# Three products of zeros ahead of each pass of the second expert layer, and the transposes of modulation sums half a piece later

## What is computed

```python
# first network, 256 tokens, four layers
for i in range(4):
    mod = cond @ ada_w[i] + ada_b[i]
    sh_a, sc_a, g_a, sh_f, sc_f, g_f = jnp.split(mod, 6, axis=-1)
    ...
    h = modulate(rms_norm(x, norm_g[i, 2]), sh_f, sc_f)
    y = jnp.square(jax.nn.relu(h @ ffn_w1[i])) @ ffn_w2[i]      # 1024 -> 4096 -> 1024
    x = x + g_f[:, None, :] * rms_norm(y, norm_g[i, 3])

# second network, expert layer (layer 0: 512 tokens, layer 1: 256 tokens)
def moe_ffn(h, w_router, e_bias, w_gate, w_up, w_down, s_gate, s_up, s_down):
    scores = jax.nn.sigmoid(h @ w_router)
    _, idx = lax.top_k(scores + e_bias, 8)
    ...
    def expert_block(args):
        tok, e = args
        xb = h_pad[tok]
        a = jax.nn.silu(xb @ w_gate[e]) * (xb @ w_up[e])        # 1024 -> 256
        return a @ w_down[e]                                    # 256 -> 1024
    ...
    return routed + shared
```

## Time and profile before

| | us |
|---|---|
| median of 3 runs | 3370.06 |
| the three runs | 3374.06, 3370.06, 3365.59 |
| the profiled execution's own time | 3373.5 |
| its span, first to last instruction | 3371.8 |
| PE busy | 3187.8 (95%) |
| DVE busy | 1277.8 (38%) |
| mean DMA rate | 255 GB/s |
| mean granted TensorE clock | 0.985 |

### The profile page before, as it was taken

One profiled execution on the slowest core, in us unless ns is written; L12 is line 12 of the kernel. 1 busy time (PEld: TensorE's weight loads), 2 busy tenths in 40 slices (PEclk: granted clock), 3 DMA queues, 4 the chain that ended last, 5 costly groups with the idle time before them and its releaser, 6 DMA issues.

```text
span 3371.8 us, 39704 instructions
## 1 busy us (share of the span) xinstructions
PE 3187.8 (95%) x14310; PEld 2152.6 (64%) x14310; DVE 1277.8 (38%) x3018; ACT 546.3 (16%) x1148; POOL 401.6 (12%) x462
## 2 busy tenths in 40 slices
PE   7999999999999999999999999998999998899897
PEld 5878878888888888888664434443445575333333
DVE  4766534565014565476442322222212033111112
ACT  3300122001021003200031211111112022111011
POOL 0000120001010000000220222221113001010000
PEclk9999999999999999999999999999999999999999
DMA  8687625774435773466300699999995216999996
GB/s 317 256 305 299 256 108 200 290 290 156 153 122 222 292 284 112 175 251 259 114 26 21 258 383 378 357 389 360 362 338 201 77 38 277 409 416 414 395 398 247
DMA packets 135329, 860.25 MB, mean 255 GB/s; under 512 B 20592, under 2 KB 24048, under 8 KB 37744
## 3 DMA queue, kind: packets, MB, share of 16 engines
q1 hardware_dynamic: 94000, 664.84, 50.2%
q0 software_dynamic: 40288, 191.41, 16.6%
q10 hardware_dynamic: 864, 1.65, 0.1%
HBM read 845.75 MB, written 35.13 MB: 261 GB/s over the span
## 4 chain that ended last, share of the span: by engine, by line
PE 76%; DMA 13%; DVE 6%; issue 2%; ACT 1%; SPq 1%; POOL 0%; POOLq 0%; DVEq 0%; ACTq 0%
PE ps L777 15%; PE ps L1179 12%; PE ps L1466 11%; DMA ring<-stream_in 10%; PE ps L1160 8%; PE ps L874 8%; PE ps L1490 6%; PE ps L1508 3%; DMA arena<-mod_stream_in 3%; DVE arena L2031 2%; PE ps L1427 1%; PE ps L789 1%; PE ps L832 1%; PE ps L841 1%; PE ps L1281 1%
## 5 line engine op out<-in xcount | busy, mean ns | idle before, releaser
L1466 PE MATMUL ps<-ring,arena 128*64 128x512 f32 (+2 forms) x2112 | 569.8, 641 | 78.0 <-DMA ring<-stream_in 76.3
L2031 DVE SCALAR_TENSOR_TENSOR arena<-arena,cond 128x512 f32<-128x512 f32 x602 | 426.7, 748 | 95.8 <-DMA arena<-mod_stream_in 86.7
L1466 PEld LDWEIGHTS ps<-ring,arena 128*64 128x64 f32 (+2 forms) x2112 | 202.9, 152 | 389.8 <-issue 385.7
L1179 PE MATMUL ps<-arena,ring 128*128 128x256 f32 x2048 | 445.1, 379 | 4.1 <-DVE arena L2353 4.1
L1179 PEld LDWEIGHTS ps<-arena,ring 128*128 128x128 f32 x2048 | 387.9, 190 | 57.1 <-issue 5.0
L1160 PE MATMUL ps<-H,ring 128*128 128x256 f32 x1920 | 420.8, 380 | 0.0
L1160 PEld LDWEIGHTS ps<-H,ring 128*128 128x128 f32 x1920 | 363.5, 190 | 48.5
L1490 PE MATMUL ps<-ring,arena 128*64 128x512 f32 (+2 forms) x1056 | 283.4, 602 | 17.2 <-issue 8.4
L1658 ACT ACTIVATE arena<-ps 128x512 f32<-128x512 f32 (+2 forms) x331 | 167.5, 506 | 720.5 <-PE ps L777 278.1
L2553 DVE TENSOR_TENSOR arena<-arena,ps 128x256 f32<-128x256 f32 x76 | 32.0, 421 | 589.4 <-ACT arena L1917 589.3
L1490 PEld LDWEIGHTS ps<-ring,arena 128*64 128x64 f32 (+2 forms) x1056 | 93.6, 144 | 178.9 <-issue 169.5
(11 more groups left out here) (290 smaller groups left out, 3156.7 us busy)
## 6 DMA issues: line engine op xcount, KB each, us to landing
ring<-stream_in SPq DMA_DIRECT2D x611, 1024.0 KB
arena<-mod_stream_in POOLq DMA_DIRECT2D x130, 1024.0 KB, 5.1
arena<-mod_stream_in SPq DMA_DIRECT2D x8, 1024.0 KB, 13.1
YS<-mod_stream_in SPq DMA_DIRECT2D x6, 1024.0 KB, 5.2
moe_out<-zeros POOLq DMA_DIRECT2D x18, 256.0 KB, 7.9
arena<-stream_in SPq DMA_DIRECT2D x4, 1024.0 KB, 5.9
stat<-stream_in SPq DMA_DIRECT2D x2, 1024.0 KB, 4.7
moe_in<-YS POOLq DMA_DIRECT2D x1, 2048.0 KB, 7.1
```

The lines of the kernel that those rows point to most:

```text
L1179: m = mm(out[:, i * T:(i + 1) * T], w[:, c * P:(c + 1) * P], f_h[:, 16 * half + c, :], start=(half == c == 0), stop=(half == 1 and c == 15))
L1466: m = mm(out[at, :], e_xt[:, k % 2, 4 * part + c, at], w[:, c * TC:(c + 1) * TC], start=(part == c == 0), stop=(part == 1 and c == 3))
L2031: ins = stt(acc, w, x, acc, MUL, ADD)
```

## The change

In the second expert layer (`if l`), each pass's `gate_up(k)` issues three products of `ones_d` by 256 columns of `zeros` into the pass's own bank. They stand behind the wait for that bank and ahead of the first wait for weights. There are 28 passes, so 84 such products.

In `ffn`, the transposes for the sums that are done beside piece j are no longer issued by PE after piece j, but between the two groups of eight products of piece j + 1. Those of the last piece of turn 0 are issued in the middle of the first piece of turn 1. Those of the last piece of turn 1 stay at its end. DVE's, ACT's and POOL's programs are the same, and so are the down layers.

```diff
             def ffn(l):
                 ph = PLAN["ffn_up", l]
 
+                def columns(j, turn):
+
+
+                    if j < 0:
+                        j, turn = 7, 0
+                    for i in up_done(l, j):
+                        mod_columns(ph, up_fill(l, j) + 1, ("up", l), i, turn)
+
                 def body(turn):
...
                                     if i == c == 0:
                                         m.then_inc(used, 1)
+                                if i == 0:
+                                    columns(j - 1, turn)
                             m.then_inc(full, 1)
-                        for i in up_done(l, j):
-                            mod_columns(ph, up_fill(l, j) + 1, ("up", l), i, turn)
+                    if not first:
+                        columns(7, turn)
                 turns(pe, ph, body, True)
...
                     for half in range(2):
                         wait_drained(pe, ph, ROWS_T + half, k)
                     out, full = bank(ph, HIDDEN, k)
+                    if l:
+                        for _ in range(3):
+                            mm(out[:, 0:T], ones_d, zeros[:, 0:T], start=True, stop=True)
                     for part in range(2):
                         views = weights(k, part)
```

## The result

The kernel with the change took 3388.94 us (median of six runs, 3385.83 to 3394.40) against 3366.45 us for the kernel before (six runs, 3365.04 to 3374.06). The ratio is 1.0061, 95% interval 1.0050 to 1.0072: 17 to 24 us slower, about 20.5. The direction was right; the loss was more than three times as large, and the median is 2 us above the range, into which the interval (3383 to 3391) reaches.

The account below looks back on a forecast made before the run. PE and the weight stream were taken to hold each other in the second expert layer, PE alone to bound the feed-forward layers. 3373.5 + 11 - 5.2 = 3379.3, less 3.4 to the median, gave 3376 us, range 3363 to 3387.

Parts of the forecast that it names:

- The rival in which the zeros are hidden: Second expert layer: the stream keeps its pace and only the moved transposes show, 3365 us; chance 0.25 with a half-hidden 3370.
- The price of a set: Head of each second-expert-layer pass: three products of zeros cost PE 1.29 us, 36.2 us over 28 passes.
- The lateness at each link: Transfers ending PE's weight waits: each issues late by the sets of three zero products before it, up to 9.0 us.
- The cover: Same transfers: time from issue to landing above a 4.9 us floor hides lateness, 0.8 to 4.0 us each.
- the term for the links: Second expert layer: lateness beyond cover, summed over the chain of transfers that end PE's waits, 13.1 us lost.
- part 1: Zeros in the second expert layer: 11 us lost, between 5.9 and 13.1, with 3 us more above.
- the cover is no cover: Second expert layer: every set between waits counts, 32 us less 5, 3397 us; lesser form 3384; chance 0.2.
- The clock: Seven waits of four-expert passes: low clock costs 18 us of PE; recovery could cut the 13.1 us loss to 5.9.
- The transposes in layers 1 to 3: Feed-forward layers: PE's waits for DVE shrink, 3.2 us gained in layers 1 and 2, 1.0 in layer 3.
- The transposes in layer 0: Feed-forward layer 0: 1 us gained, ends -1 and +2, from waits of 0.84, 3.40, 0.84 and 1.49 us.
- The sum: Whole kernel: 3373.5 + 11 - 5.2 = 3379.3, less 3.4 us for the profiled execution's height above the median: 3376 us.
- part 2: Transposes of modulation sums half a piece later in the feed-forward layers: 5.2 us gained, ends 2 and 8.

Follow-up runs that it names:

- e10_half: Kernel before with only half of each second-layer expert piece transferred: 3325.87 us against 3368.74, ratio 0.9874.
- e1_zeros: Kernel before plus only the three products of zeros at the head of each of the 28 passes: 3388.19 us against 3369.27, ratio 1.0054.
- e11_half_zeros: Kernel before with half of each second-layer expert piece transferred and three products of zeros per pass: 3357.27 us, ratio 0.9971.
- e4_rest: Kernel before plus three products of zeros in the 21 passes other than 12 to 18: 3377.59 us, ratio 1.0026.
- e6_one: Kernel before plus one product of zeros at the head of each of the 28 passes: 3373.29 us, ratio 1.0015.
- e2_columns: Kernel before with only the transposes of modulation sums moved half a piece later, no zeros: 3372.69 us, ratio 1.0007.
- e12_cols123: Kernel before with the transposes moved in layers 1, 2 and 3 only, timed a second time: 3363.97 us against 3368.2, ratio 0.9987.
- e8_cols123: Kernel before with the transposes moved in layers 1, 2 and 3 only, first timing: 3365.21 us, ratio 0.9989.

## Why the prediction was right in direction and too small

**What bounds the kernel.** Right: PE and the stream hold each other. e10_half shows what the stream is worth, e1_zeros what PE is, and e11_half_zeros that PE binds nearly alone once the stream doesn't. The rival in which the zeros are hidden, with a chance of 0.25, is out, with 18 us lost. The Trainium skill, "Perfetto Trace Analysis", section "Identifying the Most-Contended Engine", says to optimize the fullest engine first. That stands beside e10_half, where the lighter stream gained most, but it doesn't say that added work on the second engine is free, as the prediction read it: 36 us on it cost 18.

**The price of a set.** Right: 1.29 us forecast, 1.30 measured in every ordinary pass.

**The lateness at each link.** Right, by the count of sets: the table has 2.7, 5.6, 9.4, 2.5, 1.1 and 2.6 us where the count gave 3.9, 5.2, 9.0, 2.6, 1.3 and 2.6; of these only the first is off, by one set. The last link has 3.3 for a count of 5.2, which is the clock's doing (below).

**The cover: the step that failed.** "What a link has above 4.9 us is time behind other pieces, and so is its cover." This holds if the other pieces are on time. They are issued by the same SP after the same PE, so they are late too. The link to 3031.86 shows it best: cover 3.7 by the sum, but its duration shrank by 1.9 us only and stopped at 6.71, and the loss was 3.7 instead of 1.5. The kernel before has a piece near the floor in the same run of transfers. The piece issued at 2997.27, fourteen ahead of the link, lands after 5.38 us: a cover of 0.5. In the kernel after it is issued 1.8 us late (counted from the chain's first landing, as all that follows) and takes 6.74, so it lands 3.2 us late, and the link lands 3.8 late. In e1_zeros, e4_rest and e6_one that piece lands 3.2, 3.0 and 3.0 us late; in e2_columns and e12_cols123, without zeros, 1.4 and 0.8, of which the link keeps 0.5 and nothing.

The link to 3187.42 looks alike: 8.95 us from issue to landing, a cover of 4.0 by the sum, a lateness of 2.5, and its duration didn't shrink at all (9.20). In the records of the kernel before, the piece issued at 3183.86, three ahead of it, lands 5.05 us later, at 3188.90: a cover of 0.15. After it the next three land 2.49 us apart, the last at 3196.37, and that is the link. Its loss of 2.7 us stands less firmly, as the kernels without zeros have up to 1.6 there. The DMA share and rate in 40 slices of 3172 to 3202, first before, then after, show the hole at that piece (a slice is 0.75 us):

```profile
DMA  9999999999999998598999999999999999999999
GB/s 415 448 393 426 437 426 437 404 426 415 426 426 371 393 415 323 235 191 289 415 437 393 459 404 437 415 459 415 404 459 404 448 404 437 415 448 426 393 459 382
```

```profile
DMA  9999999999999999999999999999987759899999
GB/s 437 437 404 437 382 459 415 371 431 388 437 415 426 415 426 437 426 426 437 404 437 426 415 437 437 415 393 415 415 371 295 202 147 371 371 448 382 470 404 393
```

In the kernel before the rate dips to 191 GB/s near 3185, and in the kernel after to 147 near 3196: the queue ran thin ahead of the link in both. It wasn't alone. GpSimd's gather of token rows, issued at 3179.55 (3190.57 in the kernel after), falls in the same hole, and holds more of the engines than the ring does (kernel before, 3183.5 to 3184.9: packets, MB, share; q0 is the gather's queue, q1 the ring's):

```profile
q0 software_dynamic: 120, 0.23, 41.7%
q1 hardware_dynamic: 25, 0.11, 18.6%
```

How much of the hole is the gather's and how much the thin queue's, no run separates. The dip itself could have been read before the change, and so could the two pieces near the floor: in these two links the cover is that of the tightest piece in the run of landings that leads to the link, not that of the last piece.

That is read from traces; no run changed one piece alone, and it isn't the whole of it. At 3187 the least cover (0.15) explains 1.0 of the 2.7 us, and the 0.5 of the other piece 1.3 of its 3.2: the two pieces themselves then took 6.62 us where it had been 5.05, and 6.74 where it had been 5.38. The link to 3314.38 isn't a case of it either. In the kernel after, two pieces ahead of it, issued at 3314.66 and 3317.23, did reach the floor (issues of that stretch, count, KB each, median us to landing):

```profile
ring<-stream_in SPq DMA_DIRECT2D x2, 1024.0 KB, 5.0
```

But they land 2.7 and 2.5 us behind the piece ahead of them, nearly as in a full queue. The gaps are at the last two, the link among them: they take 7.86 and 7.36 us, well above the floor, and each lands 4.4 and 3.9 us behind the piece ahead of it, where the kernel before has 2.5. The stretches of the two kernels that end in this link's landing, before and after, show what that made of the stream, 1.01 of its share against 0.93:

```profile
3299.00:3321.50 22.50, 17.78 (x90) 5.68 (x86) 2.13 (x4) 1.36 (x3) 0.00 (x0) 1.00 1.01 419
```

```profile
3314.60:3338.60 24.00, 19.12 (x96) 6.73 (x92) 2.13 (x4) 1.36 (x3) 0.00 (x0) 0.98 0.93 350
```

What slows pieces that aren't alone in the queue, and by how much, stays open.

In numbers: the term for the links was 13.1 us. The losses are 19.5 in the trace of after and 15.9 in that of e1_zeros, and part 1 cost 18.2 us by the medians (13.5 to 23). The rival called "the cover is no cover" asked for 32 us, and that was too much, since the links to 2960.35 and 3245.65 did take up what they were said to.

**The clock.** The forecast took 2 us off for a clock that recovers, with 7 as the limit. The products of the passes of four in the kernel after, and the down products of the same passes in the kernel before:

```profile
L1479 PE MATMUL ps<-ring,arena 128*32 128x512 f32 x448 | 64.9, 732 | 31.6 <-DMA ring<-stream_in 31.6
L1503 PE MATMUL ps<-ring,arena 128*32 128x512 f32 x256 | 30.8, 598 | 3.9 <-DMA ring<-stream_in 2.5 <-ACT arena L1671 0.7 <-DVE slot_token L2553 0.7
```

```profile
L1490 PE MATMUL ps<-ring,arena 128*32 128x512 f32 x256 | 31.5, 610 | 7.1 <-DMA ring<-stream_in 6.4 <-ACT arena L1658 0.7
```

Against 66.6 and 31.5 that is 2.4 us, about the size taken. Inside a link it came at one place, the link to 3314.38, whose lateness is 3.3 us where four sets would make 5.2: the wait ahead had shrunk from 5.07 to 2.81 us, and the 32 records behind it took 3.57 us instead of 5.43. The rest came ahead of the first link and behind the last. That a short enough wait keeps the clock up isn't as simple as the forecast had it: behind a wait of 2.55 us, at 3166.90, the same 32 records still took 5.15 us.

**The transposes in layers 1 to 3.** Right: 4.2 us forecast (3.2 and 1.0), 3.7 and 4.2 measured, with intervals of 0.7 to 6.7 and 1.0 to 7.7; the trace of after has these three layers 4.6 us shorter.

**The transposes in layer 0.** Wrong in sign: a gain of 1 forecast, 6.4 us lost. The chain that the forecast wrote down is the one that happened: DVE waits for the transposes, POOL issues 2.6 us later, PE waits at its new place. What failed is what it was compared with. The 3.40 us wait was taken as the kernel's usual state. In e1_zeros and e8_cols123 it is 1.25 and 1.11 us, and with all that hangs on it some 3.9 us of layer 0 were this execution's alone. Against the trace of before, layer 0 of after is 2.7 us longer; against the kernel's usual 244.2 it is 6.6. The forecast also let the load take 7.2 us in both cases, while it takes 5 usually and nearly 7 when it is issued later. The sum did take off 3.4 us for the profiled execution's height above the median, without asking where it lay: by the traces it lay in this term.

**The sum.** Part 1 was 11 for a measured 18.2, part 2 was -5.2 for a measured +2.4. Both errors have one sign, and they make up 14.8 us between them: 5.8 forecast, 20.6 measured.

## What to carry to other kernels

When two engines feed each other through a ring, look for the tightest piece in the whole run of landings that leads to a wait before you call a transfer's time cover; the piece that ends the wait shows too much of it. Here about half of what was added to one engine showed, beside another at 99%. Before a wait in a profile is priced, ask whether it belongs to the kernel or to the one execution: the profiled run's height above the median is a place in the trace, and finding it tells which term it spoils. And when a step is moved later on one engine, follow who waits for it and which loads that engine's delay issues late: here the same move gained in three layers and lost in the one where the moved engine already waits for its loads.

## What was unexpected

- A 1 MB modulation load takes 5.2 us to its use when issued at 171.13 and 6.9 us when issued 2.57 us later, in the same place of the program; over the whole program the median went from 5.1 to 6.0 us (5.7 in e2_columns, with the move alone).
- Keeping PE at work in the waits for the stream brought half of the time that the low clock had cost there back (66.6 to 57.3 us), and no time that can be seen (ratio 1.0000, 3 us either way).
- A transfer with others in the queue doesn't shorten one for one when it is issued later: at 3031.86 it gave back 1.9 of 3.7 us, at 3187.42 nothing of 4.0. Added work on PE cost 42% of its length for one product per pass, 50% for three and 59% for six, with intervals that overlap.
